# A hybrid decoder step with a PEER layer on one Trainium2 core: the dense expert part on 512 tokens, the 32 sample tokens gathered

## What is computed

```python
def peer_block(hb, w_pq, peer_keys, peer_u, peer_v):
    ...
    e = jnp.take_along_axis(cidx..., fi, axis=-1)      # 8 x 16 experts per token
    g = jax.nn.softmax(fv, axis=-1)
    a = jax.nn.gelu(jnp.einsum('thkd,td->thk', peer_u[e], hb), approximate=False)
    return jnp.einsum('thk,thkd->td', (g * a), peer_v[e])
```

## Time and profile before

| | us |
|---|---|
| median of 3 executions | 3992.42 |
| lowest, highest | 3988.97, 4019.62 |
| the profiled execution | 3987.4 |
| its span, first to last instruction | 3985.6 |
| mean granted TensorE clock in it | 0.877 |

### The profile page before, as it was taken

The page is one execution under the profiler, slowest core; times in us unless marked ns, Lnnn a source line. Parts: engine busy times, 40 slices in busy tenths (PEclk is TensorE's granted clock), DMA queues, the critical chain, the costliest instruction groups (busy, mean ns, idle before and its releaser), DMA issues. The chain is left out here.

```text
span 3985.6 us, 57178 instructions
## 1 busy us (share of the span) xinstructions
PE 3195.7 (80%) x19892; PEld 2704.8 (68%) x19892; DVE 3007.7 (75%) x5897; ACT 1041.1 (26%) x1915; POOL 1578.3 (40%) x1320
## 2 busy tenths in 40 slices
PE   6654687776999986656552777999999999999997
PEld 3443344554555554336552667999999999999997
DVE  3248686885656663758998996888888888888887
ACT  2221122321222221111112553222222222223221
POOL 0035454464333332644545772333333333333332
PEclk9677897977889897778776888999999999999999
DMA  2221775687867655970000438888888888888886
GB/s 104 102 91 33 277 266 194 206 271 238 283 216 229 220 189 191 330 277 27 27 11 1 180 135 296 307 300 301 298 298 296 296 290 295 300 302 295 292 300 236
DMA packets 303822, 876.75 MB, mean 220 GB/s; under 512 B 34009, under 2 KB 125450, under 8 KB 292554
## 3 DMA queue, kind: packets, MB, share of 16 engines
q0 software_dynamic: 147456, 536.94, 39.5%
q1 hardware_dynamic: 154170, 334.15, 23.3%
q10 hardware_dynamic: 2016, 3.67, 0.3%
HBM read 819.17 MB, written 55.74 MB: 220 GB/s over the span
## 5 line engine op out<-in xcount | busy, mean ns | idle before, releaser
L109 POOL DMA_INDIRECT x_got<-v,x_expert x512 | 546.2, 1067 | 974.0 <-DVE x_y L130 874.3
L109 POOL DMA_INDIRECT x_got<-u_rows,x_expert x512 | 566.0, 1106 | 822.3 <-DVE x_got L123 703.5
L130 DVE SCALAR_TENSOR_TENSOR x_y<-x_got,x_hidden,x_y 128x1024 f32<-128x1024 f32 x512 | 665.9, 1301 | 40.8 <-DMA x_got<-v,x_expert 31.3
L123 DVE SCALAR_TENSOR_TENSOR x_got<-x_got,x_y 128x1024 f32<-128x1024 f32 x512 | 620.1, 1225 | 38.0 <-DMA x_got<-u_rows,x_expert 36.8
L1667 PE MATMUL e_a<-h2h,e_uh 128*128 128x272 f32 x2048 | 590.8, 288 | 22.1 <-DVE e_ul L1745 21.5
L1669 PE MATMUL e_a<-h2h,e_ul 128*128 128x272 f32 x2048 | 594.1, 290 | 0.0
L1684 PE MATMUL e_y<-e_wh,e_vh 128*128 128x272 f32 x2048 | 588.4, 287 | 3.6 <-DVE e_wl L1768 3.6
L1668 PE MATMUL e_a<-h2l,e_uh 128*128 128x272 f32 x2048 | 589.3, 288 | 0.0
L1685 PE MATMUL e_y<-e_wl,e_vh 128*128 128x272 f32 x2048 | 588.2, 287 | 0.0
L1686 PE MATMUL e_y<-e_wh,e_vl 128*128 128x272 f32 x2048 | 587.2, 287 | 0.0
L1667 PEld LDWEIGHTS e_a<-h2h,e_uh 128*128 128x128 f32 x2048 | 386.4, 189 | 22.9 <-issue 21.9
(11 more groups left out here) (376 smaller groups left out, 5681.4 us busy)
## 6 DMA issues: line engine op xcount, KB each, us to landing
e_u<-uT SPq DMA_DIRECT2D x128, 512.0 KB, 6.6
e_v<-v SPq DMA_DIRECT2D x64, 1024.0 KB
gates_d<-g_stage SPq DMA_DIRECT2D x8, 4352.0 KB, 11.8
e_gate<-gates_d SPq DMA_DIRECT2D x32, 1088.0 KB
d_page<-page SPq DMA_DIRECT2D x128, 144.0 KB, 2.3
d_latent<-page_rows SPq DMA_DIRECT2D x128, 128.0 KB
t0r_w<-w_pq SPq DMA_DIRECT2D x16, 512.0 KB, 3.5
x_got<-u_rows,x_expert POOLq DMA_INDIRECT x512, 5.6
```

The costliest lines, as they stand in the source:

```text
L109: pool.indirect_dma_start(out=self.got[n % RING_G][:], out_offset=None, in_=self.tables[phase], in_offset=bass.IndirectOffsetOnAxis(ap=sel ...
L123: dve.scalar_tensor_tensor(out=row[:], in0=row[:], scalar=1.0, in1=self.y[g][:], op0=ALU.mult, op1=ALU.mult, accum_out=self.hidden[:, g, k ...
L130: dve.scalar_tensor_tensor(out=self.y[g][:], in0=row[:], scalar=self.hidden[:, g, k:k + 1], in1=self.y[g][:], op0=ALU.mult, op1=ALU.add).t ...
```

## The change

Three things are changed together.

1. **The dense part holds tiles 4 to 7 only**, 512 tokens, which is one PSUM bank of float32: `DT` = 512, no halves. A row is 24 matmuls of 512 columns, a quad's `add_values` 96. `GT` is 64 (weight table of 128 groups).
2. **PSUM.** Two banks hold `a`. Of the eight output chunks five (`HELD` 0 to 4) have a bank each and accumulate over all 32 quads; chunks 5, 6, 7 (`TURNED`) share one bank in turn, and VectorE adds each to `y` before the next may begin. The order is 0, 5, 1, 6, 2, 7, 3, 4. At the end ScalarE copies the five held banks to `y`. VectorE's slots per quad are now 20: one in each of four rows, four before each of the three adds, four after the last.
3. **The sample tokens are gathered.** Their 128 picks are folded on four groups of 32 partitions, so 32 steps of `u` and 32 of `v` do for them (tile index 4, `FOLD` = 4, `FOLDED` = 32); the last 548 steps become 612. The router's query blocks are 256, 512 and 32 columns (before: 256, 272, 272). At its end SP copies gates and expert numbers of the sample tokens to the four groups with eight small DMAs, after one more small VectorE instruction. In `finish` a matmul with a folding matrix adds the four groups.

```diff
-DT = NT - GTOK
-NB = 2
-TD = DT // NB
-GT = 68
+DT = SEQ - GTOK
+GT = 64
 GB = DT // GT
 PICKS = H * TOPK
+FOLD = P // NS
+FOLDED = PICKS // FOLD
+ROWS = (TG - TA) * P
...
+        self.picks = [PICKS] * TG + [FOLDED]
...
+        folds = t1 == TILES
+        own = range(g0, g1 + 1) if folds else range(g0, g1)
+        if folds:
+            sample = sb("c_sample", [NS, PICKS], U32)
...
+        turned = range(TG - t0, PT_TILES - t0) if folds else ()
...
+                for c in range(FOLD):
+                    sp.dma_start(gather.y[TG][c * NS:(c + 1) * NS, :], a["h2_d"][SEQ:NT, :]).then_inc(s["c_h2"], 16)
...
+                sp.wait_ge(s["c_gate"], H)
+                sp.wait_ge(s["c_sample"], 1)
+                for c in range(FOLD):
+                    some = slice(c * FOLDED, (c + 1) * FOLDED)
+                    rows = slice(c * NS, (c + 1) * NS)
+                    sp.dma_start(gather.gate[rows, TG, 0:FOLDED], out[0:NS, 0, T - 1, some]).then_inc(s["c_fold"], 16)
+                    sp.dma_start(gather.expert[rows, TG, 0:FOLDED], sample[:, some]).then_inc(s["c_fold"], 16)
+                sp.wait_ge(s["c_fold"], 32 * FOLD)
...
-            for n, t in enumerate(range(g1 - t0, T)):
+            for n, t in enumerate(turned):
...
+                dve.scalar_tensor_tensor(out=sample[:], in0=out[0:NS, 1, T - 1, :], scalar=float(NK),
+                                         in1=out[0:NS, 2, T - 1, :], op0=ALU.mult,
+                                         op1=ALU.add).then_inc(s["c_sample"], 1)
+            dve.wait_ge(s["c_h2"], 16 * (G + 1) + (16 * FOLD if folds else 0))
+            for g in own:
                 dve.tensor_tensor(gather.y[g][:], gather.y[g][:], gain[:], ALU.mult).then_inc(s["c_scaled"], 1)
...
-    YBANKS = 8 - NB
     QUADS = NK // 4
     U_RING = 4
+    HELD = (0, 1, 2, 3, 4)
+    TURNED = (5, 6, 7)
+    ORDER = (0, 5, 1, 6, 2, 7, 3, 4)
+    YT = len(TURNED)
...
-        wf = [sb(f"e_wf{b}", [P, TD]) for b in range(NB)]
+        wf = [sb(f"e_wf{b}", [P, DT]) for b in range(2)]
         wh = [sb(f"e_wh{r}", [P, DT], F32R) for r in range(5)]
         wl = [sb(f"e_wl{r}", [P, DT], F32R) for r in range(5)]
-        a_b = [ctx.enter_context(nc.psum_tensor(f"e_a{r}", [P, 512], F32)) for r in range(NB)]
-        y_b = [ctx.enter_context(nc.psum_tensor(f"e_y{r}", [P, 512], F32)) for r in range(YBANKS)]
+        a_b = [ctx.enter_context(nc.psum_tensor(f"e_a{r}", [P, DT], F32)) for r in range(2)]
+        held = [ctx.enter_context(nc.psum_tensor(f"e_y{k}", [P, DT], F32)) for k in HELD]
+        turned = ctx.enter_context(nc.psum_tensor("e_yt", [P, DT], F32))
...
+        MADE, ADDED = 4, 4
+        SLOTS = 4 + MADE * YT + ADDED
         left = len(gather.order) - gather.planned
         def steps_through(slot):
             return (slot * left + QUADS * SLOTS - 1) // (QUADS * SLOTS)
...
-                for b in range(NB):
-                    after(pe, s["e_gelu"], NB * j + b - NB + 1)
-                    o = a_b[b][:, 0:TD]
-                    cols = slice(b * TD, (b + 1) * TD)
-                    for k in range(KD):
-                        pe.matmul(o, uh[q][:, k, :], h2h[:, k, cols], start=k == 0, stop=False)
-                        pe.matmul(o, uh[q][:, k, :], h2l[:, k, cols], start=False, stop=False)
-                        mm = pe.matmul(o, ul[q][:, k, :], h2h[:, k, cols], start=False, stop=k == KD - 1)
-                    mm.then_inc(s["e_a"], 1)
-
-            def add_values(m, slots):
+                after(pe, s["e_gelu"], j - 1)
+                o = a_b[q][:, :]
+                for k in range(KD):
+                    pe.matmul(o, uh[q][:, k, :], h2h[:, k, :], start=k == 0, stop=False)
+                    pe.matmul(o, uh[q][:, k, :], h2l[:, k, :], start=False, stop=False)
+                    mm = pe.matmul(o, ul[q][:, k, :], h2h[:, k, :], start=False, stop=k == KD - 1)
+                mm.then_inc(s["e_a"], 1)
+
+            def add_values(m, slots, first, last):
...
+                pe.wait_ge(s["e_wl"], 4 * m + 4)
+                for k in ORDER:
+                    if k in HELD:
+                        o, begins, ends = held[HELD.index(k)][:, :], first, last
+                    else:
+                        after(pe, s["e_yadd"], YT * m + TURNED.index(k))
+                        o, begins, ends = turned[:, :], True, True
+                    for c, r in enumerate(slots):
+                        h, l = vh[:, c, k * P:(k + 1) * P], vl[:, c, k * P:(k + 1) * P]
+                        pe.matmul(o, h, wh[r][:, :], start=begins and c == 0, stop=False)
+                        pe.matmul(o, h, wl[r][:, :], start=False, stop=False)
+                        mm = pe.matmul(o, l, wh[r][:, :], start=False, stop=ends and c == 3)
+                    mm.then_inc(s["e_y"], 1)
+
+            def body(i, first, last):
...
+                act.wait_ge(s["e_a"], j + 1)
+                after(act, s["e_wl"], j - 1)
+                act.activation(wf[j % 2][:], a_b[j % 2][:, :], ACT.Gelu).then_inc(s["e_gelu"], 1)
+                act.wait_ge(s["e_wf"], j + 1)
+                act.activation(wh[slot][:], wf[j % 2][:], ACT.Copy).then_inc(s["e_wh"], 1)
...
+            act.wait_ge(s["e_y"], KD * QUADS)
+            for k in HELD:
+                act.activation(y[:, k, :], held[HELD.index(k)][:, :], ACT.Copy).then_inc(s["e_out"], 1)
...
+                dve.wait_ge(s["e_gelu"], j + 1)
+                w3 = wf[j % 2][:].rearrange("p (b t) -> p b t", t=GT)
+                dve.tensor_tensor(w3, w3, gate[g][:, :, part, :], ALU.mult).then_inc(s["e_wf"], 1)
+                row_step()
+                dve.wait_ge(s["e_wh"], j + 1)
+                dve.tensor_tensor(wl[slot][:], wf[j % 2][:], wh[slot][:].bitcast(F32),
+                                  ALU.subtract).then_inc(s["e_wl"], 1)
+
+            def add(m, first, row_steps):
+                for n, k in enumerate(TURNED):
+                    row_steps(MADE * n, MADE)
+                    dve.wait_ge(s["e_y"], KD * m + ORDER.index(k) + 1)
+                    after(dve, s["e_yadd"], YT * m)
+                    if first:
+                        dve.tensor_copy(y[:, k, :], turned[:, :]).then_inc(s["e_yadd"], 1)
+                    else:
+                        dve.tensor_tensor(y[:, k, :], turned[:, :], y[:, k, :], ALU.add).then_inc(s["e_yadd"], 1)
+                row_steps(MADE * YT, ADDED)
+
+            def row_steps(slot, count=1):
+                gather.step(dve, steps_through(slot + count) - steps_through(slot))
...
+                        row_steps(at + q)
                     if q == 3:
-                        add(2 * i + h, i == 0 and h == 0, lambda n: row_steps(SLOTS * (2 * i + h) + 4 * NB + n))
+                        add(2 * i + h, i == 0 and h == 0, lambda n, count: row_steps(at + 4 + n, count))
...
+            dve.wait_ge(s["e_out"], len(HELD))
...
+            pe.wait_ge(s["z_add"], 2 * (PT_TILES - 1))
+            for c in range(2):
+                mm = pe.matmul(bank[PT_TILES % 2][0:NS, c * 512:(c + 1) * 512], fold[:],
+                               gather.y[TG][:, c * 512:(c + 1) * 512], start=True, stop=True)
+            mm.then_inc(s["z_tr"], 1)
...
-    u = [("u", g, k) for k in range(PICKS) for g in range(TA, TG)]
+    own = [(g, k) for k in range(PICKS) for g in range(TA, TG + 1) if k < (FOLDED if g == TG else PICKS)]
+    u = [("u", g, k) for g, k in own]
     both = [step for pair in zip(rest, u) for step in pair]
     n = min(len(rest), len(u))
-    return both + rest[n:] + u[n:] + [("v", g, k) for k in range(PICKS) for g in range(TA, TG)]
+    return both + rest[n:] + u[n:] + [("v", g, k) for g, k in own]
...
+                    if t == PT_TILES:
+                        return (h2h, h2l)[k][:, :, ROWS:ROWS + NS]
...
-                    blocks = [(0, late, (h2h, h2l), 0)] + [(late + b * TD, TD, dense, b * TD) for b in range(NB)]
+                with nc.sbuf_tensor("picks", [P, 3, DT], F32) as picks:
+                    blocks = [(0, ROWS, (h2h, h2l), 0), (ROWS, DT, dense, 0), (ROWS + DT, NS, (h2h, h2l), ROWS)]
...
+        "fold": np.tile(np.eye(NS, dtype=f), (P // NS, 1)),
```

More of the change, by code:

```diff
@@ L86, in __init__ @@
         self.y = [sb(f"x_y{g}", [P, D]) for g in range(TA)]
[L87 to L89 removed]
+        self.hidden = sb("x_hidden", [P, TG + 1, PICKS])
+        self.gate = sb("x_gate", [P, TG + 1, PICKS])
+        self.expert = sb("x_expert", [P, TG + 1, PICKS], U32)
+        self.picks = [PICKS] * TG + [FOLDED]
         names = " ".join(f"x_got{k}" for k in range(RING_G))
@@ L1592, in experts @@
         block = ctx.enter_context(nc.Block())
-        YB = NB * KD
         SLOT = (0, 1, 2, 3, 4, 1, 2, 3, 0)
-        GBB = GB // NB
-        def freed(m, n):
-            before = n - YBANKS
-            if before < 0:
-                before = max(q for q in range(YB) if q % YBANKS == n) - YB
-            return YB * m + before + 1
-        SLOTS = 4 * NB + YB
+        MADE, ADDED = 4, 4
+        SLOTS = 4 + MADE * YT + ADDED
```

(55 more changed lines are left out.)

69 lines of the change are left out of this document (31 added, 38 removed).

## The result

| | before | after |
|---|---|---|
| median of 18 executions each, us | 4011.2 | 3974.3 |
| lowest, highest | 3985.4, 4021.1 | 3941.1, 3989.1 |
| ratio, with its 95% interval | | 0.990 (0.988 to 0.992) |
| the profiled execution | 3987.4 | 3974.9 |
| its mean granted clock | 0.877 | 0.862 |

The change makes the kernel 1.0% faster, some 37 us. I had forecast 3874, 113 us less than the profiled execution, with a range of 3800 to 3960: the sign was right, the size three times too large, and the measured time lies above the range.

The account below looks back on a forecast made before the run. TensorE's matmul columns were taken to bound the dense part. From 3987.4: dense part -112, gate matrix -13.5, router +4 and +4, end of dense part +3, last part +1, giving 3874 us; range 3800 to 3960.

Parts of the forecast that it names:

- The matmul's price: Dense part: a 512-column matmul at full clock takes 0.216 us, so a quad's matmuls take 41.4 us instead of 48.0.
- my upper bound: Dense part: 0.2255 us per 512-column matmul, if the 12 ns over columns/2.4 stay; the lower bound was 0.2145.
- The waits: Dense part: TensorE waits for VectorE's adds of turned chunks, behind grouped gather steps, making the 41.4 us quad 44.5.
- the second rival: Dense part: every matmul keeps the extra 12 ns (0.2255 us); quad 45.4 with 2.1 of waits, kernel 3903; chance 13%.
- the part of my count about the ring: Dense part: five gather buffers refill too slowly for grouped steps, one issue per 1.5 us, so VectorE's adds come late.
- The 12 ns stay: Dense part: every matmul keeps 12 ns over columns/2.4, 0.2255 us; quad 45.4, 83 us saved, kernel 3903; chance 13%.
- The ring covers the groups: Dense part: gathered rows land in time for grouped steps; quad 42.4, 179 us saved, kernel 3807; chance 20%.
- The ring starves: Dense part: step pitch above 1.82 us makes quads exceed 48.0; at 2.0 quad 50.7, kernel 4072; chance 12%.
- The gate table: Dense part: the table's 256 KB row pitch halves its DMA rate, 80 us over the forecast, kernel 3954; chance 6%.
- Gate matrix: Gate matrix stage: 128 groups of four tokens for 136, VectorE needing 1.69 us each, saves 13.5 us.
- router: Router: +4 us for query matmuls in 512 and 32 columns, +4 for eight small DMAs at its end.
- end of the dense part: After the last dense matmul: five ScalarE copies of 0.6 us replace one short add, +3 us.

## Why the prediction was wrong

**The matmul's price** is the step that failed, and 66 of the 71 us that the dense part is short: (0.2267 - 0.216) x 192 matmuls x 32 quads. In the term "I take 0.216, nearest to the 512-column row" I had 13 ns at 256 and 12 at 272 columns, both float32r, and 1 ns at 512, from float32 matmuls that pass twice. I read a trend with length into a difference of type: two lengths 6% apart show no trend at all, and the third row was another kind of instruction. The same-type rows gave 0.2255, my upper bound, and I chose the one whose column count was nearest. The run with bfloat16 shows both prices side by side in one kernel, 0.2160 and 0.2270, so the 11 ns are not something that only a short matmul fails to cover. What in float32r takes them stays open; it isn't the traffic of the gathers (no steps) or the length of the weight load (half the columns), and it is absent at half clock.

**The waits** came out at 3.3 us a quad where I had 3.1, and that is luck. My count with the group of steps and the single bank gives 2.1 at the true price of a matmul (the second rival). The records divide the 3.3 so: 2.6 are TensorE's waits (from start to start; as idle time the view has 68 us, 2.2 a quad), 0.3 are 48 matmuls at half clock, in six groups that each begin within 1.5 us of the end of a wait of 1.8 to 2.0 us, which I had named as a risk; and 0.5 lie in starts further apart than 0.227 without idle time in the view, which no row explains. The profile after looked as I had said it would, with TensorE waiting 2 to 3 us a quad, nearly all on the add of the turned chunks; yet spreading the steps or doubling the bank, from which I then expected 44.5 to 45.5, changed nothing (46.7, 47.0). What holds is the part of my count about the ring. I had a buffer's issue 0.3 us after it is free, or 1.5 to 1.9 behind the last issue, and the landing 5.7 after it; the medians are 1.1 from free to issue and 6.0 to the landing. How much of the 1.2 us beyond my count each of them makes isn't shown; seven buffers leave 1.0 of the whole 3.3.

**The rivals.** The 12 ns stay (3903): right in kind, yet 1.5 us a quad short, 0.2 of it the price (0.2267 for 0.2255) and 1.2 the waits and what goes with them. The ring covers the groups (3807): false, VectorE waits 120 us for rows. The ring starves (s above 1.82): not here; it is what four buffers do, at 50.6 us a quad and +2.6 over before. The gate table (3954) lies nearest to the measured time, by chance: its packets take what they took (1088 bytes in 49.3 ns before, 1024 in 48.6 after, means in the dense part), and the stretch from its store to the dense part got 1.9 us shorter. The Trainium skill's 207 GB/s (DMA: Bandwidth & Descriptors, "Latency and other measured facts") is of copies between HBM tensors; my 401 was of loads into SBUF, over 2 us, so the two do not contradict each other.

**The small terms.** Gate matrix -13.3 (forecast -13.5), router +8.2 (+8), end of the dense part +3.6 (+3, five copies of 0.607 us each). VectorE's work was 38.0 us a quad in the forecast; in the inner stretch it is busy 1004 of 1200, 39 a quad. The DMA's share was right too: 342 GB/s is what the seven-buffer kernel moves at 44.5 us a quad, so the forecast of 44.5 describes the better kernel, but by two errors that cancel, with 2.1 us of matmul price added and 2.1 of waits taken away.

## What to carry to other kernels

Take a matmul's price only from rows of the same data type (look it up in the source, as the profile prints one name for two types), and a dependence on length only from lengths far apart; a term that is multiplied by 6144 deserves its own bound in the forecast, not a choice. When an edit packs the users of a ring of buffers into groups, compare the round trip of a buffer (free to issue, issue to landing, use) with the number of buffers times the pitch of the steps, that is the time from one step to the next. When TensorE's wait names an add or a split, ask first whether the whole queue behind it is late, and try one or two more buffers before moving the work about.

## What the hardware showed that I had not expected

- A 512-column float32r matmul takes 0.2267 us at full clock and 0.4267 at half; a bfloat16 one, on constants, 0.2160 at full clock. One bfloat16 matmul between two float32r ones makes three cost 0.693 in place of 0.680.
- GpSimd's issue of an indirect DMA takes 0.94 us when VectorE pauses, 0.94 to 2.0 (mean 1.4) beside two gather steps in a row, and 3.0 beside the split of `u` and then of `v` (24 such issues after the change); the mean in the dense part rose from 0.97 to 1.33. The Trainium skill (GPSIMD Engine Reference, "1. Specifications") has the two engines share an SBUF interface, with contention when a VectorE instruction has two inputs in SBUF; the steps and the splits have two. The means agree; single issues do not all: the one at 3043.07 takes 0.94 beside a whole step. No run here took that alone away.
- Half the bytes shorten the landing of a gather only from 6.0 to 3.8 us.
